# Experts' blocks gate their rows and add them into the residual by an accumulating scatter

## What is computed

```
x = x + g1 * m                                   # residual: "x2" in the kernel
h = rmsnorm(x, norm2_w) * (1 + sc2) + sh2        # input of the experts: "h2"
w_top = jax.nn.softmax(top_l, axis=-1) * p_sel[:, None]     # two experts and two weights for a row
out = (silu(xb @ w_gate[e]) * (xb @ w_up[e])) @ w_down[e]   # per block of rows of one expert
y = segment_sum(out * rows_w[:, None], rows_tok)            # the two weighed outputs of a row, added
x = x + g2 * y                                   # g2: one row of 1024 per request group
y_prompt = rmsnorm(x, final_norm_w) * (1 + sc) + sh
```

## Time and profile before

| | |
|---|---|
| median of 3 runs | 3184.86 us (3182.17 to 3193.7) |
| profiled execution, its own time | 3192.89 us |
| its span in the profile | 3191.3 us |
| PE busy | 78% of the span |
| DVE busy | 44% |
| POOL busy | 10% |
| granted TensorE clock, mean | 0.881 of full speed |
| HBM read, written | 291.64 MB, 109.46 MB |

### The profile page before, as it was taken

One profiled execution on the slowest core, in us unless ns is written; L12 is line 12 of the kernel. 1 busy time (PEld: TensorE's weight loads), 2 busy tenths in 40 slices (PEclk: granted clock), 3 DMA queues, 4 the chain that ended last, 5 costly groups with the idle time before them and its releaser, 6 DMA issues. The chain is left out here.

```text
span 3191.3 us, 37481 instructions
## 1 busy us (share of the span) xinstructions
PE 2502.9 (78%) x12087; PEld 1905.9 (60%) x12088; DVE 1389.8 (44%) x2636; ACT 982.0 (31%) x1659; POOL 308.5 (10%) x314
## 2 busy tenths in 40 slices
PE   7769999829999188787978589942999999999700
PEld 1168888718999155454545368832878878877500
DVE  0158888750000143444434356560235551344568
ACT  0034444321111133332323333320224441234422
POOL 0000000000000200000000000013111221112123
PEclk9989999959999588898878789976999999999855
DMA  6621111123543613233330244332345661454476
GB/s 238 234 88 70 65 71 71 40 96 118 187 175 106 159 31 82 61 72 72 71 72 7 71 162 139 131 123 93 108 143 186 237 233 67 141 188 176 172 260 223
DMA packets 201025, 401.98 MB, mean 126 GB/s; under 512 B 66552, under 2 KB 87318, under 8 KB 197340
## 3 DMA queue, kind: packets, MB, share of 16 engines
q1 hardware_dynamic: 182124, 347.25, 34.1%
q0 software_dynamic: 18832, 53.90, 4.9%
HBM read 291.64 MB, written 109.46 MB: 126 GB/s over the span
## 5 line engine op out<-in xcount | busy, mean ns | idle before, releaser
L1218 PE MATMUL c_po<-c_pr,c_vv 128*66 128x512 f32 (+2 forms) x720 | 323.6, 534 | 13.1 <-ACT c_pr L1269 13.1
L1269 ACT ACTIVATE c_pr<-c_ps,c_nf 128x512 f32<-128x512 f32 (+2 forms) x360 | 206.2, 593 | 356.9 <-PE c_ps L1210 356.5
L1287 DVE TENSOR_REDUCE c_mx<-c_pm 128x1 f32<-128x512 f32 (+3 forms) x304 | 177.8, 614 | 216.3 <-PE c_pm L1190 157.9
L1190 PE MATMUL c_pm<-c_km,c_q 66*128 66x512 f32 (+1 forms) x336 | 183.9, 601 | 73.3 <-DMA c_vv<-in_cache_v_dram 38.3
L267 PE MATMUL b_ps<-b_h_hi,wb_hi 128*128 128x256 f32 x576 | 164.4, 285 | 39.3 <-DMA b_h_lo<-h_lo 39.3
L1204 PE MATMUL c_ps<-c_q,c_k 128*128 128x512 f32 (+2 forms) x360 | 189.0, 525 | 0.0
L1026 DVE TENSOR_TENSOR b_qk_lo<-b_qk,b_qk_hi 128x2048 fp32r<-128x2048 f32 x11 | 25.2, 2293 | 333.9 <-ACT b_qk_hi L988 333.9
L269 PE MATMUL b_ps<-b_h_hi,wb_lo 128*128 128x256 f32 x576 | 163.5, 284 | 0.0
L268 PE MATMUL b_ps<-b_h_lo,wb_hi 128*128 128x256 f32 x576 | 163.5, 284 | 0.0
L1190 PEld LDWEIGHTS c_pm<-c_km,c_q 66*128 66x128 f32 x336 | 73.8, 226 | 144.2 <-DVE c_mx L1287 66.0
L267 PE MATMUL p_zx<-wa_hi,ah_hi 128*128 128x432 f32 x408 | 155.2, 380 | 3.6 <-DVE ah_lo L646 3.6
(11 more groups left out here) (359 smaller groups left out, 5651.9 us busy)
## 6 DMA issues: line engine op xcount, KB each, us to landing
x_raw_g<-in_w_gate_dram SPq DMA_DIRECT2D x32, 1024.0 KB, 7.4
x_raw_u<-in_w_up_dram SPq DMA_DIRECT2D x32, 1024.0 KB, 12.4
x_raw_d<-in_w_down_dram SPq DMA_DIRECT2D x32, 1024.0 KB, 6.5
wa<-in_w_ada_dram SPq DMA_DIRECT2D x12, 2048.0 KB, 7.9
z_y<-y_tok SPq DMA_DIRECT2D x32, 512.0 KB, 5.1
c_k<-k_hi SPq DMA_DIRECT2D x16, 672.0 KB
h_hi<-ah_hi SPq DMA_DIRECT2D x17, 512.0 KB, 2.6
h_lo<-ah_lo SPq DMA_DIRECT2D x17, 512.0 KB, 3.5
```

The costliest lines, as they stand in the source:

```text
L1190: last = pe.matmul(p_m[x % 2][:, 0:w * P], q2[0:KR, s, u["tile"] * P:(u["tile"] + 1) * P], km[:, s, kc], start=True, stop=not masked)
L1218: pe.matmul(p_o[it["chunk"] % 2][0:VW, cols], vv[:, it["s"], key_tile(it), :], pr[:, i % RING, cols], start=it["first"], stop=it["last"]). ...
L1269: act.activation(pr[:, n % RING, cols], p_s[n % NPS][:, cols], ACT.Exp, bias=nf[:, it["s"], kt:kt + 1]).then_inc(exp_done, 1)
L1287: dve.tensor_reduce(mx[:, unit, pc["x"]:pc["x"] + 1] if many else nm[:, unit:unit + 1], p_m[n % 2][:, 0:pc["nk"] * P], AX.X, ALU.max, nega ...
```

## The change

In routing, a slot of `c.slot_tok` grows from 2 numbers to 4: the row to gather, the row of x2 to which the result goes, the row's weight as raw bits, and the index of the g2 row of its request group. `y_tok` is gone; x2 gets 128 spare rows, which are set to zero. SP also loads the four modulation rows that the last stage needs (`c.last_rows`).

In experts, POOL's `scatter` now loads the list, waits for it, gathers for each of the 128 rows its g2 row into `x_gate2` by an indirect load, waits for that to land, waits for `x_out`, and scatters with `compute_op=ALU.add` into x2. DVE takes both halves out of `x_pd`, in one operation each that multiplies by the row's weight and by `x_gate2`. ACT takes out nothing. `x_to`, `x_gate2`, `x_out` and `x_rows` are single buffers.

In final, a tile is loaded once (from x2), ACT squares and takes the root, DVE scales and shifts, SP stores. Four buffers; POOL does nothing.

```diff
@@ routing, sync
+            sp.dma_start(c.x2[TP:, :].rearrange("p (j d) -> p j d", d=P), c.zeros[:].unsqueeze(1).to_broadcast([P, KD, P])).then_inc(spare_zeroed, 16)
+            for g in range(2):
+                for r, m in enumerate((M_SCF, M_SHF)):
+                    sp.dma_start(c.last_rows[:, g, r, :], mod_row(c, g, m)).then_inc(rows_loaded, 16)
@@ routing, vector
+            then(dve.tensor_copy(tok[:, :, :, 2].bitcast(F32), wt))
@@ experts, gpsimd, scatter(n)
                 pool.dma_start(to[:], c.slot_tok[bass.ds(n * P, P), :]).then_inc(to_loaded, 16)
                 pool.wait_ge(to_loaded, n * 16 + 16)
-                pool.wait_ge(out_act, n + 2)
-                pool.wait_ge(out_dve, n + 2)
                 pool.sem_inc(gather_go, 1)
-                nc.gpsimd.indirect_dma_start(out=c.y_tok, out_offset=bass.IndirectOffsetOnAxis(ap=to[:, 1:2], axis=0),
-                                             in_=out[:], in_offset=None).then_inc(stored, 16)
+                nc.gpsimd.indirect_dma_start(out=gate2[:], out_offset=None, in_=c.mod_dram.rearrange("(r j) p -> r (j p)", j=KD),
+                                             in_offset=bass.IndirectOffsetOnAxis(ap=to[:, 3:4], axis=0)).then_inc(gate2_loaded, 16)
+                pool.wait_ge(gate2_loaded, n * 16 + 16)
+                pool.wait_ge(out_taken, n * 2 + 4)
+                pool.sem_inc(gather_go, 1)
+                nc.gpsimd.indirect_dma_start(out=c.x2, out_offset=bass.IndirectOffsetOnAxis(ap=to[:, 1:2], axis=0),
+                                             in_=out[:], in_offset=None, compute_op=ALU.add).then_inc(stored, 16)
@@ experts, scalar
-            def take_out(n):
-                act.wait_ge(d_done, n * 2 + 1)
-                act.wait_ge(out_free, n + 1)
-                act.activation(out[:, 0:512], p_d[:, 0:512], ACT.Copy).then_inc(out_act, 1)
@@ experts, vector
             def take_out(n):
-                dve.wait_ge(d_done, n * 2 + 2)
                 dve.wait_ge(out_free, n + 1)
-                dve.tensor_copy(out[:, 512:1024], p_d[:, 512:1024]).then_inc(out_dve, 1)
+                dve.wait_ge(gate2_loaded, n * 16 + 16)
+                for half in range(2):
+                    cols = slice(half * 512, half * 512 + 512)
+                    dve.wait_ge(d_done, n * 2 + 1 + half)
+                    dve.scalar_tensor_tensor(out=out[:, cols], in0=p_d[:, cols], scalar=to[:, 2:3].bitcast(F32), in1=gate2[:, cols],
+                                             op0=ALU.mult, op1=ALU.mult).then_inc(out_taken, 1)
@@ final, sync
+            def load(i):
+                n = rows_of(i)
+                if i >= RING:
+                    sp.wait_ge(scaled, i - RING + 1)
+                sp.dma_start(x3[0:n, i % RING], c.x2[i * P:i * P + n, :]).then_inc(x_loaded[i % RING], 16)
+            for i in range(NT):
+                sp.wait_ge(out_ready, i + 1)
+                dst = a["y_prompt"][0, i * P:(i + 1) * P, :] if i < NT_P else a["y_sample"][0]
+                sp.dma_start(dst, out[0:rows_of(i), i % RING]).then_inc(stored[i % RING], 16)
+                if i + RING < NT:
+                    load(i + RING)
@@ final, vector
-                dve.scalar_tensor_tensor(out=t[:, s, :], in0=y2[:, s, :], scalar=c.weight[:, bass.ds(i * 2 + 1, 1)], in1=y1[:, s, :], op0=ALU.mult, op1=ALU.add).then_inc(y_weighed, 1)
-                dve.tensor_tensor(t[:, s, :], t[:, s, :], rows[:, group, 0, :], ALU.mult).then_inc(y_gated, 1)
```

More of the change, by code:

```diff
@@ L2114, in final @@
-        y_loaded, x2_loaded, stored = ([sem(f"{w}{s}") for s in range(2)] for w in ("y_loaded", "x2_loaded", "stored"))
+        x3, out, junk = sb("x3", [P, RING, D]), sb("out", [P, RING, D]), sb("junk", [P, 2, D])
+        st = sb("st", [P, NT, 4])
+        ssq, ms, root, rs, scaled, out_ready = map(sem, ("ssq", "ms", "root", "rs", "scaled", "out_ready"))
+        x_loaded, stored = ([sem(f"{w}{s}") for s in range(RING)] for w in ("x_loaded", "stored"))
         block = ctx.enter_context(nc.Block())
-        LAST = NT - 1
+        rows_of = lambda i: P if i < NT_P else DEC
@@ L2118, in _ @@
+        group_of = lambda i: 0 if i < NT_P else 1
         @block.sync
         def _(sp):
[L2120 to L2130, removed]
@@ new lines, in load @@
+            def load(i):
[3 more added lines that the diff above has]
+                sp.dma_start(x3[0:n, i % RING], c.x2[i * P:i * P + n, :]).then_inc(x_loaded[i % RING], 16)
+            for i in range(RING):
+                load(i)
+            for i in range(NT):
[4 more added lines that the diff above has]
+                    load(i + RING)
@@ L2172, in _ @@
+            for s in range(RING):
+                sp.wait_ge(stored[s], 16 * len(range(s, NT, RING)))
         @block.scalar
@@ L2174, in _ @@
             load_functions(nc, act, SQRT)
-            def weigh(i, s, count):
-                act.wait_ge(y_loaded[s], count * 32)
-                act.sem_inc(weigh_go, 1)
-                act.activation(y1[:, s, :], y1[:, s, :], ACT.Copy, scale=c.weight[:, bass.ds(i * 2, 1)]).then_inc(y1_weighed, 1)
-            def one(i, s):
-                act.wait_ge(x3_ready, i + 3)
-                act.activation(junk[:], x3[:, s, :], ACT.Square, accum_out=st[:, s, 0:1]).then_inc(ssq, 1)
-                act.wait_ge(ms, i + 1)
-                act.activation(st[:, s, 2:3], st[:, s, 1:2], ACT.Sqrt).then_inc(root, 1)
@@ L2187, in _, with square @@
[L2187 to L2193 removed]
+            def square(i):
+                n = rows_of(i)
+                act.wait_ge(x_loaded[i % RING], 16 * (i // RING + 1))
+                act.activation(junk[0:n, i % 2], x3[0:n, i % RING], ACT.Square, accum_out=st[0:n, i, 0:1]).then_inc(ssq, 1)
@@ L2195, in _, with take_root @@
+            def take_root(i):
+                n = rows_of(i)
+                act.wait_ge(ms, i + 1)
+                act.activation(st[0:n, i, 2:3], st[0:n, i, 1:2], ACT.Sqrt).then_inc(root, 1)
+            square(0)
+            for i in range(NT):
+                if i + 1 < NT:
+                    square(i + 1)
+                take_root(i)
         @block.vector
         def _(dve):
-            dve.sem_inc(y_weighed, 2)
-            dve.sem_inc(scaled, 2)
-            dve.wait_ge(rows_loaded, 16 * 6)
@@ L2241 @@
+            mean(0)
+            for i in range(NT):
+                if i + 1 < NT:
+                    mean(i + 1)
+                normalize(i)
 class Shared:
```

127 lines of the change are left out of this document (33 added, 94 removed).

## The result

The changed kernel takes 3265.84 us, the median of 4 runs (3259.96 to 3285.39), beside 3183.53 for the kernel before (4 runs). The ratio is 1.026 with a 95% interval of 1.021 to 1.031: 82 us slower. The direction was forecast, the size was not: +37 us, with 3265 as the upper end of the forecast's own range, which the median just passes.

A forecast was written before the change was run, and what follows sets the result against it. The experts were taken as bound by PE, the last stage as held mostly by DVE. Terms -82 + 1 + 2 + 116 = +37 on 3184.9 gave 3222 us; own range 3200 to 3265, 8 in 10 within 3135 to 3320.

The forecast's parts named there:

- The last stage: Final stage: DVE only scales and shifts each tile and traffic shrinks; 66 us instead of 148.3, saving 82 us.
- Routing and the ends: Routing: extra small operations and loads, +1 us; the last scatter's own latency, +2 us.
- Quiet turns: 16 turns of POOL's loop away from expert changes: 18.3 us each instead of PE's 18.05, slack used up, +17 us.
- x: Experts, each turn: the accumulating scatter's extra HBM reads delay the next gather by 1.5 us, bounded by 0 and 3.4.
- Last blocks: 12 turns in an expert's last block, g2 gather beside weight loads: 24.5 us each, 294 against 253, +41 us.
- about L+12.5 beside weights (with 1 us for the list): Turns beside weight loads: `x_gate2` is there about 12.5 us after `x_tok`'s issue, with 8.54 us for the gather.
- First blocks: 10 turns in an expert's first block, DVE waiting for `x_gate2`: 22.6 us each, 226 against 178, +48 us.
- One-block experts: 3 turns in experts of one block: second half on DVE and more traffic, some 3 us each, +10 us.
- the hiding gather: Rival in experts: g2 gather avoids collision with weights and the scatter's reads cost nothing; -49 us, 3136 us, chance 0.25.
- A slow accumulate: Rival in experts: accumulating scatter costs 3.4 us, 1.9 more in each of 41 turns, +78, 3300 us; chance 0.2.
- Break even: Rival in experts: scatter's extra near 1 us and half the collision, about +80 against -82 + 3; 3185 us, chance 0.13.
- DMA as the bound: Rival in experts: 44 MB more traffic raises DMA share from 0.48 to 0.62; not binding by itself, no chance given.

The follow-up runs named there:

- not added: The changed kernel with a plain storing scatter in place of the accumulating one, so the sum is missing from its output: 3198.38 us, ratio 1.003.
- no g2 gather: The changed kernel with the prompt's g2 row loaded once for all rows instead of gathered, sample rows' g2 missing: 3156.65 us, ratio 0.988.
- lists kept: The changed kernel with all lists loaded into SBUF once at the stage's start and copied from there each turn, order unchanged: 3183.67 us, ratio 0.999.
- turned kernel: The changed kernel with its lists in SBUF and POOL's gather of the next rows ahead of g2 gather and scatter: 3120.63 us, ratio 0.980.

## Why the prediction went wrong in size

The terms, worked out as in the prediction, over the same classes of turns (sums in us):

| turns | before | forecast | measured | not added | no g2 gather | lists kept |
|---|---|---|---|---|---|---|
| quiet, 16 | 276 | 293 | 308 | 286 | 290 | 293 |
| last block, 12 | 253 | 294 | 314 | 285 | 247 | 260 |
| first block, 10 | 178 | 226 | 239 | 220 | 202 | 211 |
| one-block experts, 3 | 81 | 91 | 90 | 85 | 88 | 91 |
| all 41 | 788 | 904 | 951 | 876 | 827 | 855 |

- **The last stage** (forecast 66 us, -82): right. 65.6 us, -82.7; the scaling takes 1.28 us. DVE is busy 46.2 us of it at 264 GB/s, so the term was sized rightly, by the traffic as well.
- **Routing and the ends** (+3): right, +3.1.
- **Quiet turns** (18.3 each): 19.25. The mechanism was right: `take_out` ends at L+9.5 on average (9.3 forecast). The step that fell short is x, "1.5" behind the 7.5. From `take_out`'s end to L are 9.8 us on average, 7.6 where nothing is added: x is 2.2. The forecast's 1.5 was worked out from bytes alone. The later landing is 1.5 us, the size that the bytes gave, though no run shows that bytes are its cause; what is missing is that POOL needs 0.64 us longer to issue such a scatter. +15 us in all, of which x is 11 and small shortfalls of the 9.3 and the 7.5 the rest.
- **Last blocks** (24.5 each): 26.2. The step that failed is "about L+12.5 beside weights (with 1 us for the list)". It puts the gather's issue at L+4.0. It is at L+6.25 on average, because the list lands late while the weights load (DMA share 0.97 in the window above, 0.04 in the quiet turn). The gather beside weights was sized rightly (9.0 us from issue to `take_out` at 2325.53, 8.5 on average, 8.5 forecast). `take_out` ends at L+16.2 instead of 13.9, the part behind it is 0.6 shorter than forecast, which hides part of the error: +20 us. This is the largest single error, and that the list decides is shown by the kernel with lists kept, where these turns fall by 4.5 us each.
- **First blocks** (22.6 each): 23.85. `take_out` ends at L+9.65 (9.3 forecast), and from there to L are 14.2 us (13.3 forecast, x with it): the scatter's issue, beside DVE's split of the down weights, takes 2.35 us on average. +12 us.
- **One-block experts** (+10): +8.

Together +46 us on the forecast of +116 for the stage. The working bounded x by 0 and 3.4, which holds the 2.2; it gave the list beside weights no bounds. And it read `take_out` in quiet turns of the kernel before from one turn (L+9.9); over all 16 it starts at L+8.9, so the slack was 2.8 us on average and not 3.8. The sum did not use this.

The rivals: the hiding gather needed x below 0.3 and a collision below 1 us, and both were far from it. A slow accumulate of 3.4 would have given 3300; at x = 2.2 it is about a third of the way. Break even needed x near 1 and half of the collision. DMA as the bound is refuted twice, by its share of 0.54 in the stage and by the turned kernel, which moves the same bytes at PE's pace. The Trainium skill's rule for one DMA (DMA: Bandwidth & Descriptors, section Anatomy of one DMA) would have made the first-block turns 1.7 us shorter, and so missed by more; the g2 gather in the quiet turn has `x_gate2` there 4.2 us after its issue (2256.94 to 2261.14), between that page's 3.2 and the 4.93 of the earlier trace rows. The other rule, which the Trainium skill states for the reducing step of a collective (Collectives: The Full Stack, Part 3), half the rate for two source reads, agrees with the 1.5 us by which the next landing is later, and says nothing of the issue.

## What to carry to other kernels

When an edit puts a chain of transfers (list, gather, scatter) behind one another on one engine, price the smallest of them by what is in flight at the moment of its issue, and not by its size: a list of 2 KB was waited for 2 us in a quiet turn and 5 to 8 behind or beside large transfers, and keeping the lists in SBUF was worth 82 us of the kernel. Load such lists once, if they fit. And before turning an order so that the critical gather goes first, ask what feeds that gather: in the changed kernel the turned order was worth nothing with lists in HBM and 63 us with lists in SBUF.

## What the runs showed of the hardware

**An accumulating scatter** of 128 rows of 4 KB takes GpSimd 1.65 us to issue, beside 1.01 us for a storing one, and makes the gather behind it land 1.5 us later. The scatter itself lands 6.3 us after its issue instead of 3.4 (medians of 43), in every kernel of this study that has it (6.3 to 6.5 in eight) or not (3.4 in six).

**GpSimd beside VectorE's two-input operations.** In the kernel with lists kept, the same copy of 128 x 4 numbers takes 0.18 us elsewhere (2334.31) and 1.49 and 2.25 us (2310.50 and 2311.93, shown above) while VectorE subtracts the weights' high parts:

```profile
2309.65 4.50 DVE L2062 TENSOR_TENSOR x_g_lo<-x_raw_g,x_g_hi 128x2048 fp32r<-128x2048 f32 x2 [1.11 <-ACT x_g_hi L2009]
2334.31 0.18 POOL L1886 COPY x_tok<-x_lists 128x4 int32 x1 [5.67 <-DMA x_rows<-h,x_tok]
```

An accumulating scatter's issue goes from 1.65 to 3.45 us at such a place (2303.72 in the turned kernel, where VectorE's subtraction runs from 2303.38 to 2307.86). The Trainium skill says that GpSimd's SBUF interface is shared with VectorE, with contention at instructions with two SBUF inputs (GPSIMD Engine Reference, section 1, Specifications); the trace agrees.

**TensorE's clock.** In the changed kernel PE stood idle for 7.91 us ahead of a first block's rows. Windows of PE's idle time, of what followed, of a piece of that, and of the stretch after it:

```profile
2329.00:2336.40 7.40, 0.66 (x3) 0.66 (x4) 0.00 (x0) 0.00 (x0) 1.45 (x3) 0.59 0.66 142
2336.40:2344.00 7.60, 7.60 (x29) 6.29 (x28) 1.72 (x3) 1.20 (x2) 2.09 (x3) 0.72 0.20 70
2337.20:2339.70 2.50, 2.50 (x9) 2.02 (x8) 1.38 (x2) 0.89 (x2) 0.48 (x1) 0.50 0.06 2
2344.00:2348.00 4.00, 4.00 (x18) 3.20 (x18) 2.42 (x3) 3.20 (x2) 1.65 (x1) 1.00 0.00 0
```

After the rows have come the granted clock is 0.50, its lower level (1.2 GHz), and matmuls of 512 columns last 0.63 us in PE's timeline; from 2340.79 on they last 0.40, and the last window has the full clock (2.4 GHz). Over the stage the clock went from 0.99 to 0.92, and PE was busy 798 us instead of 760 with the same matmuls. In this turn nearly nothing of it is on the path: `take_out` waits 4.59 us for `x_gate2` and its second half 0.31 us for PE (2343.66, 2344.72). How much the clock cost in the other turns was not measured by itself. The rise in PE's busy time here, with the same matmuls, is the lower clock and not more work.
